# Single-use buffers for four expert loads, and all adaLN loads inside the trunk

## The chip, the cores and the metric

One core of a Trainium2 chip runs the whole kernel. The metric is device microseconds of one execution. TensorE (PE) multiplies, VectorE (DVE), ScalarE (ACT) and GpSimd (POOL) do the rest, SyncE (SP) issues most of the DMAs, and 16 DMA engines carry them.

## The reference

One layer of a diffusion backbone in fp32, width 2048, on two streams of 128 tokens each (context and latent):

```python
mods = silu(c) @ w_ada + b_ada                 # 2048 -> 6 x 2048, for both streams
h = rmsnorm(x, norm1_g) * (1 + sc1) + sh1
u_f, q, k, v, g_a, g_b = h @ w_in + b_in       # 2048 -> 8192
merged = sigmoid(g_a) * (fourier(u_f) @ w_fourier) + sigmoid(g_b) * (attention(q, k, v) @ w_na_o)
x1 = x + ga1 * (merged @ w_out)
h2 = rmsnorm(x1, norm2_g) * (1 + sc2) + sh2
# router: best of 4 groups, then the best 2 of its 4 experts; 16 experts in all
y = sum_e comb[:, e] * ((silu(h2 @ w_g[e]) * (h2 @ w_u[e])) @ w_d[e])
x2 = x1 + ga2 * y
out = rmsnorm(x2, final_norm_g)                # and k, v of the context stream
```

## The kernel before

**The trunk.** All weights are read once, in loads of 1 MB. The dense weights (w_in, w_na_o, w_fourier, w_out) are 96 loads, `l` = 0 to 95; each is two units of 12 matmuls (`unit`, L776): a weight is split into a high and a low part (ScalarE `high` L1302, VectorE `low` L1652, four units ahead), and hi*hi, lo*hi and hi*lo are added up for both samples. Loads 80 to 95 are w_out (`L_OUT` = 80). After each chunk of four of these VectorE (`read_chunk`, L1743) multiplies by the adaLN gate (`gab`), adds to `x1`, and makes `yt`. The adaLN weights are another 96 loads; 0 to 31 go another way, 32 to 95 are *groups* `ada_super(a)` (L760) of four matmuls, eight instructions in the profile, that add into bank 7. The loads of both kinds share a ring of four 1 MB buffers, `raw`, in the order of `ring_order` (L350). From load 18 on TensorE runs two groups after the first unit of every second load. `LATE_ADA = 5` (L346) keeps the last five groups, 91 to 95, out of this: they come last in the ring, ScalarE issues their loads during the last loads of the trunk (L1500, and L1525 for 95), and TensorE runs them in the seam.

**The seam** lies between the last matmul of load 95 and the first expert matmul. TensorE, from L1042: router matmuls of block 2 for both samples, transposes of `x1` for block 3 and sample 0, group 91, transposes for sample 1, router matmuls of block 3, groups 92 and 93, the rank matmuls (they wait for VectorE's `chosen`), groups 94 and 95. VectorE: gate product and sum for sample 0, then sample 1 (both wait for the whole load, L1748), `yt`, the inverse root mean square, the logits, `chosen`, `token_low(3)` for both samples (L1804, the low part `t_lo` of the tokens), the slot keys and `rounds` (how many rounds of 64 tokens an expert needs), the first `pick` tiles (L2041), and then, after group 95, the gate row `garow`. TensorE reads `rounds` into a register, waits for `pick` and all eight `t_lo`, and makes the slot rows (L1091) and the gathered tokens `xg` (L1080).

**The experts.** 16 experts in 8 pairs. Each pair has 16 gate/up loads (four quarters q, gate and up, two experts) and 8 down loads; 192 loads in all, numbered n = 0 to 191 in the order of use, unit u using loads 2u and 2u + 1. Loads 0 to 15 are the gate/up loads of pair 0. The first unit of its quarter 3 is unit 6, with loads 12 and 13. Eleven buffers (`MRAW`) are used in turn: slots 0 to 3 lie over `w_hi` and `w_lo`, 4 to 7 over `raw`, 8 to 10 are `mraw_g`, `mraw_x`, `mraw_y`. Load n goes to slot n mod 11 once load n - 11 has been used (`slot_free`, L512). TensorE raises `loads_used` when a load has been used.

SyncE issues all of these in program order, so whatever it waits for holds up everything behind it: loads 9 and 10 as soon as it is through with the trunk's loads, 8 after chunk 21, 0 and 2 after load 94 of the trunk, 1 and 3 after load 95, 4 to 7 when the four `raw` buffers are free of groups 92 to 95, then the value of `rounds`, and loads 11 to 191 by `slot_free`. At the end of its loop it waits for all eleven slots, and then issues the output's DMAs.

Regions of SBUF: A (32 KB a partition) holds `m_hi` and `m_lo` during the output projection, and then `xg`, `d_hi`, `d_lo`, `hidT`, `sg`, `hid`; F (32 KB) holds `x1`, and over its upper half `x1T` (the router's operand) and later `ga2b`.

## Time and profile before

| | us |
|---|---|
| median of 3 runs | 1212.66 |
| lowest, highest | 1212.19, 1212.76 |
| the profiled execution, its own time | 1213.01 |
| its span | 1211.2 |
| TensorE busy | 1125.0 (93%) |
| VectorE busy | 535.5 (44%) |
| ScalarE busy | 365.2 (30%) |
| data moved | 423.22 MB, mean 349 GB/s |

A busy TensorE is not one at its peak: matmul ends are modelled, and one that waits for nothing follows the one before it without a gap. In the windows of the rows below the columns are: stretch and its length, busy us and number of instructions of PE, PEld (weight load), DVE, ACT and POOL, then the granted TensorE clock as a share of 2.4 GHz, the mean busy share of the 16 DMA engines, and GB/s. In a timeline line the columns are start, duration, engine, source line, operation, output <- inputs, shapes, and the number of instructions merged. A "q" behind an engine is its sequencer, which issues DMAs. "Chain" is the work that ended last, followed back from the end.

### The profile page before, as it was taken

How to read it: one execution, taken by the hardware profiler on the slowest of the kernel's cores; microseconds unless marked ns; L12 is line 12 of the kernel's file. 1: busy time of each engine (PE TensorE's matmuls, PEld its weight loads, DVE VectorE, ACT ScalarE, POOL GpSimd, SP SyncE). 2: the span in 40 equal slices, each digit the busy share in tenths (PEclk: the TensorE clock that was granted, in tenths of full speed). 3: DMA queues.
4: the chain of work that ended last, by engine and by line, in shares of the span. 5: the costliest groups of instructions: out<-in, count | busy, mean ns of one | idle time of the engine just before them, and what ended most of it. 6: DMA issues, size and time to landing. Idle time of an engine off the chain costs nothing.

```text
span 1211.2 us, 14465 instructions
## 1 busy us (share of the span) xinstructions
PE 1125.0 (93%) x5577; PEld 686.6 (57%) x5577; DVE 535.5 (44%) x781; ACT 365.2 (30%) x512; POOL 54.7 (5%) x100
## 2 busy tenths in 40 slices
PE   5899999999999999999999999999999888988795
PEld 2575766777777777677788865443334233423231
DVE  0364575555455444454557654133324141514046
ACT  3342342444433333333345533311112011201023
POOL 0210100110000210000011100000000000000000
PEclk9899999999999999999999999899999999999998
DMA  9999978888877898888898798899999999999994
GB/s 359 384 386 374 361 263 321 295 293 287 286 281 284 308 351 322 310 316 314 317 331 260 225 367 360 363 422 423 423 423 422 423 423 422 423 423 424 423 411 171
DMA packets 114964, 423.22 MB, mean 349 GB/s; under 512 B 9088, under 2 KB 9264, under 8 KB 82640
## 3 DMA queue, kind: packets, MB, share of 16 engines
q1 hardware_dynamic: 101824, 388.52, 82.2%
q0 software_dynamic: 5424, 15.35, 4.9%
q10 hardware_dynamic: 7648, 18.42, 4.3%
q8 instruction: 45, 0.74, 0.2%
q14 instruction: 23, 0.19, 0.0%
HBM read 418.27 MB, written 3.98 MB: 349 GB/s over the span
## 4 chain that ended last, share of the span: by engine, by line
PE 66%; DMA 29%; DVE 2%; SPq 1%; issue 1%; ACT 1%; DVEq 0%
PE bank L791 13%; PE bank L793 13%; PE bank L792 12%; PE bank L1139 10%; DMA mraw<-in_w_exp_up 6%; PE bank L772 4%; DMA raw<-in_w_in 4%; DMA raw<-in_w_ada 4%; DMA mraw<-in_w_exp_gate 3%; PE bank L1169 3%; PE bank L1080 2%; DMA mraw_x<-in_w_exp_up 2%; DMA mraw_g<-in_w_exp_up 2%; DMA mraw_y<-in_w_exp_gate 2%; DMA mraw_g<-in_w_exp_down 2%; DMA mraw_y<-in_w_exp_up 2%
## 5 line engine op out<-in xcount | busy, mean ns | idle before, releaser
L1657 DVE TENSOR_TENSOR w_lo<-raw,w_hi 128x1024 fp32r<-128x1024 f32 x192 | 231.9, 1223 | 256.3 <-ACT w_hi L1310 255.0
L1310 ACT ACTIVATE w_hi<-raw 128x1024 fp32r<-128x1024 f32 x192 | 200.3, 1057 | 322.2 <-DMA raw<-in_w_in 160.9
L791 PE MATMUL bank<-w_hi,h_hi 128*128 128x512 f32 x512 | 206.9, 404 | 7.1 <-DVE uqkv L1740 5.7
L1139 PE MATMUL bank<-mraw,xg 128*64 128x512 f32 x768 | 193.9, 602 | 15.9 <-DMA mraw<-in_w_exp_gate 8.1
L792 PE MATMUL bank<-w_lo,h_hi 128*128 128x512 f32 x512 | 200.6, 392 | 0.0
L793 PE MATMUL bank<-w_hi,h_lo 128*128 128x512 f32 x512 | 200.2, 391 | 0.0
L1139 PEld LDWEIGHTS bank<-mraw,xg 128*64 128x64 f32 x768 | 61.9, 138 | 118.8 <-issue 114.2
L791 PEld LDWEIGHTS bank<-w_hi,h_hi 128*128 128x128 f32 x512 | 96.7, 189 | 47.9 <-issue 15.7
L793 PEld LDWEIGHTS bank<-w_hi,h_lo 128*128 128x128 f32 x512 | 96.5, 189 | 21.0
L792 PEld LDWEIGHTS bank<-w_lo,h_hi 128*128 128x128 f32 x512 | 96.7, 189 | 18.3
L1169 PE MATMUL bank<-mraw,hidT 128*64 128x512 f32 x320 | 83.3, 596 | 16.2 <-DMA mraw<-in_w_exp_down 13.8
L2112 DVE SCALAR_TENSOR_TENSOR d_lo<-bank,slot_w,d_hi 128x512 fp32r<-128x512 f32 x32 | 23.9, 747 | 160.3 <-ACT d_hi L1603 159.6
L1603 ACT ACTIVATE d_hi<-bank,slot_w 128x512 fp32r<-128x512 f32 x32 | 22.0, 688 | 229.0 <-PE bank L1169 142.0
L2124 DVE TENSOR_TENSOR bank<-bank,ga2b 128x512 f32<-128x512 f32 x64 | 41.5, 694 | 80.0 <-PE bank L1210 79.9
L772 PE MATMUL bank<-raw,cpad 128*32 128x512 f32 x512 | 63.5, 606 | 4.5 <-DMA raw<-in_w_ada 4.5
L1169 PEld LDWEIGHTS bank<-mraw,hidT 128*64 128x64 f32 x320 | 26.7, 137 | 60.5 <-issue 56.1
L791 PE MATMUL bank<-w_hi,m_hi 128*128 128x512 f32 x128 | 50.9, 398 | 0.0
L793 PE MATMUL bank<-w_hi,m_lo 128*128 128x512 f32 x128 | 50.0, 390 | 0.0
L792 PE MATMUL bank<-w_lo,m_hi 128*128 128x512 f32 x128 | 49.9, 390 | 0.0
L756 PE MATMUL bank<-araw,cpad 128*32 128x512 f32 x256 | 35.1, 657 | 13.6 <-DMA araw<-in_w_ada 13.6
L2059 DVE TENSOR_TENSOR xg<-bank,rbi 128x512 f32<-128x512 f32 x32 | 21.9, 685 | 52.9 <-PE bank L1080 52.9
L1139 PE MATMUL bank<-mraw_x,xg 128*64 128x512 f32 x88 | 40.0, 597 | 1.8 <-DMA mraw_y<-in_w_exp_gate 1.6
(283 smaller groups left out, 1311.0 us busy)
## 6 DMA issues: line engine op xcount, KB each, us to landing
raw<-in_w_in SPq DMA_DIRECT2D x64, 1024.0 KB, 8.8
raw<-in_w_ada SPq DMA_DIRECT2D x59, 1024.0 KB, 7.5
mraw<-in_w_exp_up SPq DMA_DIRECT2D x49, 1024.0 KB, 20.9
mraw<-in_w_exp_gate SPq DMA_DIRECT2D x47, 1024.0 KB, 20.9
mraw<-in_w_exp_down SPq DMA_DIRECT2D x40, 1024.0 KB, 20.8
araw<-in_w_ada SPq DMA_DIRECT2D x64, 512.0 KB, 10.4
raw<-in_w_out ACTq DMA_DIRECT2D x12, 1024.0 KB, 9.2
raw<-in_w_na_o SPq DMA_DIRECT2D x8, 1024.0 KB, 8.1
```

The costliest lines, as they stand in the source:

```text
L756: last = nc.tensor.matmul(bank[7 - b % 2][32 * g:32 * g + 32], cpad[:, 2 * j + g % 2], araw[:, n % ARAW, g], start=j == 0, stop=j == 7)
L772: last = nc.tensor.matmul(bank[7][32 * g:32 * g + 32], cpad[:, k], raw[:, n % RAW, g], start=k == 0, stop=k == KD - 1)
L791: nc.tensor.matmul(o, hi[:, k, s], wh, start=k == first, stop=False)
L792: nc.tensor.matmul(o, hi[:, k, s], wl, start=False, stop=False)
L793: last = nc.tensor.matmul(o, lo[:, k, s], wh, start=False, stop=k == final)
L1080: last = nc.tensor.matmul(out[:, kk * EPG * CAP:(kk + 1) * EPG * CAP], (t_hi, t_lo)[part][:, s, k * P:(k + 1) * P], pick[:, s, g * EPG:(g ...
L1139: last = nc.tensor.matmul(out[x * CAP:(x + 1) * CAP], xg[:, q * LOAD_K + kk, e * CAP:(e + 1) * CAP], slab(slot)[:, kk * COL:(kk + 1) * COL ...
L1169: last = nc.tensor.matmul(bank[first_bank + n][x * CAP:(x + 1) * CAP], hidT[:, i % 2, k, x * CAP:(x + 1) * CAP], slab(slot)[:, n * COL:(n ...
L1310: nc.scalar.activation(w_hi[:, u % AHEAD], r, ACT.Copy).then_inc(hi_ready, 1)
L1657: v.tensor_tensor(w_lo[:, u % AHEAD], r, w_hi[:, u % AHEAD].bitcast(F32), ALU.subtract).then_inc(raw_done[n % RAW], 4)
L2112: v.scalar_tensor_tensor(out=d_lo[:, c % 2], in0=bank[first_bank + n][:], scalar=slot_w[:, i:i + 1], in1=d_hi[:, c % 2].bitcast(F32), op0= ...
L2124: v.tensor_tensor(bank[out + s][:], bank[out + s][:], ga2b[:, s, cols], ALU.mult).then_inc(y_scaled, 1)
```

## The change

1. `LATE_ADA` becomes 0. Groups 91 to 95 run inside the trunk: two groups after the first unit of loads 76, 78 and 80 (before: one, 90, at load 76 and none later). ScalarE issues no adaLN load any more.
2. The last dense load (95) is multiplied by `last_load`: all twelve matmuls of sample 0, then all of sample 1, each raising `unit_used` by one. VectorE's product for each sample waits for its own half.
3. TensorE's order in the seam: transposes of block 3, sample 0; router of block 2; transposes for sample 1; router of block 3; rank matmuls.
4. `token_low(3)` is split: sample 0 ahead of the rank reduction, sample 1 behind the first `pick` tiles.
5. Loads 8 to 11 go to four buffers that are used once: two in A + 16 KB (over `m_lo`, free after load 93 and load 95), two in F + 16 KB (over `x1T`, free after the router). They count their landing on the semaphores of `part_landed`. All other loads have a *place* in the ring (n below 8, else n - 4); place p waits for the load at place p - 11.
6. SyncE's order: 13, 14, 12 (after chunk 21), 8 (after load 93 of the trunk), 4 to 7 (after the conversions of dense loads 92 to 95), 0 and 2, 1 and 3, 9, then 10 and 11 after the router, the value of `rounds`, 15, and the rest as before.
7. At the end of its loop SyncE first waits for the last of ScalarE's squares (`x2_squared`), then for the eleven places.
8. `cmp` moves from A + 24 KB to A.

```diff
+        mraw_a = place("mraw_a", [P, 2, LOAD_K * COL], A + 16 * KB)
+        mraw_f = place("mraw_f", [P, 2, LOAD_K * COL], F + 16 * KB)
-        cmp = place("cmp", [P, NS * 5, EPG, 2 * EPG], A + 24 * KB)
+        cmp = place("cmp", [P, NS * 5, EPG, 2 * EPG], A)
-        LATE_ADA = 5
+        LATE_ADA = 0
+        ONCE, ONCE_AT = 4, 2 * RAW
+        def single_use(n):
+            return ONCE_AT <= n < ONCE_AT + ONCE
+        def place_in_ring(n):
+            return n if n < ONCE_AT else n - ONCE
+        def load_at(place):
+            return place if place < ONCE_AT else place + ONCE
...
             def slot_free(r, n):
-                if n >= MRAW:
-                    sp.wait_ge(loads_used, used_value(r, n - MRAW))
+                place = place_in_ring(n)
+                if place >= MRAW:
+                    sp.wait_ge(loads_used, used_value(r, load_at(place - MRAW)))
...
-                first_gate_up_load(2 * RAW + 1)
-                first_gate_up_load(2 * RAW + 2)
+                first_gate_up_load(13)
+                first_gate_up_load(14)
                 sp.wait_ge(chunk_read, reads(21))
-                first_gate_up_load(2 * RAW)
+                first_gate_up_load(12)
+                sp.wait_ge(unit_used, 2 * L_ALL - 4)
+                first_gate_up_load(8)
+                for n in range(RAW):
+                    sp.wait_ge(raw_done[n], 8 * (RING_LOADS // RAW))
+                    first_gate_up_load(RAW + n)
                 for n in (0, 2, 1, 3):
                     sp.wait_ge(unit_used, 2 * L_ALL - 2 + n % 2 * 2)
                     first_gate_up_load(n)
-                for n in range(RAW):
-                    sp.wait_ge(raw_done[n], 8 * (RING_LOADS // RAW))
-                    first_gate_up_load(RAW + n)
+                first_gate_up_load(9)
+                sp.wait_ge(route_done, NS)
+                first_gate_up_load(10)
+                first_gate_up_load(11)
                 sp.wait_ge(rounds_ready, 1)
                 sp.reg_load(rounds_end, rounds[0:1, 0:1])
-                slot_free(r, MRAW)
-                first_gate_up_load(MRAW)
-                for up in range(2):
-                    gate_up_loads(r, 0, 3, up)
+                slot_free(r, 15)
+                first_gate_up_load(15)
...
+                sp.wait_ge(x2_squared, r * 8 + 8)
+                sp.sem_inc(slots_freed, 1)
...
+            last_load(L_ALL - 1)
+            x1_transposes(3, 0)
             for s in range(NS):
                 router(2, s)
-            x1_transposes(3, 0)
-            ada_super(91)
             x1_transposes(3, 1)
             for s in range(NS):
                 router(3, s).then_inc(route_done, 1)
-            for a in (92, 93):
-                ada_super(a)
             pe.wait_ge(chosen_ready, 1)
...
-            for a in (94, 95):
-                ada_super(a)
...
-                if L_ALL <= l + RAW < L_ALL + LATE_ADA:
-                    ada_super_load(act, 96 - LATE_ADA + l + RAW - L_ALL)
...
-            ada_super_load(act, 95)
...
-                dve.wait_ge(unit_used, 2 * l + 2)
+                dve.wait_ge(unit_used, 2 * l + 2 - (l == L_ALL - 1))
...
-            token_low(3)
+            token_low(3, (0,))
...
             build_pick(0, EPG)
+            token_low(3, (1,))
```

## Rows read from the trace of the kernel before

**Rows 1.** The page: GB/s that the DMA engines moved, in 40 slices.

```profile
GB/s 359 384 386 374 361 263 321 295 293 287 286 281 284 308 351 322 310 316 314 317 331 260 225 367 360 363 422 423 423 423 422 423 423 422 423 423 424 423 411 171
```

**Rows 2.** Windows by stage: length, busy us by engine, clock, DMA share, GB/s.

```profile
600.00:700.00 100.00, 100.00 (x471) 83.28 (x470) 66.67 (x73) 51.19 (x62) 9.64 (x18) 1.00 0.85 278
...
766.00:844.00 78.00, 78.00 (x387) 32.20 (x385) 24.55 (x38) 17.27 (x30) 0.00 (x0) 1.00 1.00 414
844.00:1187.00 343.00, 301.75 (x1381) 119.38 (x1379) 105.88 (x168) 44.63 (x75) 0.00 (x0) 1.00 1.01 421
```

**Rows 3.** The chain of waits (start us, us, what) from the seam on.

```profile
713.21 7.16 DMA raw<-in_w_ada
720.41 1.98 PE bank L772 x8
...
727.80 7.09 PE bank L1139 x32
...
754.83 4.45 PE bank L1251 x32
...
844.23 17.08 DMA mraw<-in_w_exp_up
```

**Rows 4.** SyncE: its DMA issues (start us, us, what), the first expert loads.

```profile
702.45 0.33 SPq L509 DMA_DIRECT2D mraw<-in_w_exp_gate  x1
...
751.49 0.33 SPq L509 DMA_DIRECT2D mraw_g<-in_w_exp_up  x1
752.00 0.33 SPq L509 DMA_DIRECT2D mraw_x<-in_w_exp_gate  x1
...
755.43 10.96 SPq L509 DMA_DIRECT2D mraw<-in_w_exp_up  x2
...
766.06 0.33 SPq L509 DMA_DIRECT2D mraw<-in_w_exp_up  x1
```

**Rows 5.** Windows around load 23, columns as above.

```profile
764.00:766.00 2.00, 2.00 (x12) 0.62 (x10) 0.00 (x0) 0.00 (x0) 0.00 (x0) 0.92 0.06 25
```

**Rows 6.** TensorE in the trunk: a timeline row, two windows, a row of waits.

```profile
580.67 1.92 PE L772 MATMUL bank<-raw,cpad 128*32 128x512 f32 x16
...
594.67:613.85 19.18, 19.18 (x89) 15.87 (x86) 14.40 (x18) 8.10 (x8) 0.00 (x0) 1.00 0.84 311
569.55:593.67 24.12, 24.12 (x116) 18.28 (x113) 9.25 (x9) 9.17 (x9) 0.00 (x0) 1.00 0.91 328
...
PE bank L772 <- DMA raw<-in_w_ada: 4.5, 4, 1.7
```

**Rows 7.** Timeline of the seam; idle time before it in brackets.

```profile
708.85 0.69 DVE L1781 TENSOR_TENSOR gab<-gab,bank 128x512 f32<-128x512 f32 x1 [9.47 <-PE bank L793]
...
710.18 0.68 DVE L1781 TENSOR_TENSOR gab<-gab,bank 128x512 f32<-128x512 f32 x1
...
716.77 1.93 DVE L1804 TENSOR_TENSOR t_lo<-yt,t_hi 128x512 fp32r<-128x512 f32 x2
...
718.61 0.19 DVE L2027 TENSOR_REDUCE rt<-bank 128x16 f32<-128x32 f32 x1
...
719.68 0.75 DVE L2041 TENSOR_TENSOR pick<-cst_route,key 128x256 fp32r<-128x256 f32 x2
...
722.28 1.22 PE L1091 MATMUL bank<-pick,rr 128*128 128x256 f32 x4
```

**Rows 8.** Windows where the granted clock fell, and before the first.

```profile
716.00:720.00 4.00, 2.03 (x18) 0.90 (x14) 3.79 (x13) 0.45 (x2) 0.00 (x0) 1.00 0.96 320
720.00:723.40 3.40, 2.99 (x13) 1.32 (x14) 1.38 (x4) 0.00 (x0) 0.00 (x0) 0.50 0.98 410
...
757.50:764.30 6.80, 6.80 (x23) 3.43 (x25) 0.00 (x0) 2.41 (x6) 0.00 (x0) 0.50 0.88 360
```

**Rows 9.** Timeline of the end: last square, first output DMA.

```profile
1201.13 0.19 ACT L1584 ACTIVATION_READ_ACCUMULATOR sg<-x 128x1 f32 x1
...
1204.20 0.36 SPq L581 DMA_DIRECT2D out<-x  x1
```

64 lines of the change are left out of this document (43 added, 21 removed).

## The prediction

> **What bounds the kernel now.** I read the page's slices first: data moves at 225 to 386 GB/s in the first 26 slices and stands at 422 to 424 GB/s from slice 27 nearly to the end [rows 1]. The stages say which side is the limit. From 600 to 700 us TensorE is busy all of the time and the DMA engines move 278 GB/s: the trunk is TensorE's. From 844 to 1187 us the DMA engines have a share of 1.01 at 421 GB/s and TensorE idles 41 of 343 us: the experts are the load stream's [rows 2]. The chain of waits shows the same turn: up to 844 us it is TensorE back to back, broken at one place in the seam by an adaLN load (713.21, 7.16 us) with the matmuls of its group behind it, and from 844.23 it hops from one expert load to the next [rows 3]. One load of 1 MB (1.0486 MB) at 421 GB/s is 2.49 us.
>
> So two things can move the end: the number of bytes still to fetch after the moment at which the stream last ran dry, and that moment. It can be found. SyncE issued load 22 at 755.43 and load 23 at 766.06, one wait of 10 us between them; load 23 reuses the buffer of load 12, so it waits for unit 6, the first of the two units of the pair's last quarter [rows 4]. The DMA engines meanwhile ran out: share 0.06 from 764 to 766 us [rows 5], against 1.00 in the stage from 766 to 844 and 1.01 in the one after it [rows 2]. Hence the **anchor**: end = end of unit 6 (766.0) + 169 loads (23 to 191) + the tail. 766.0 + 169 x 2.49 = 1187, which is where the stream ends.
>
> **The change part by part.**
>
> *Five adaLN groups into the trunk.* Before, groups 91 to 95 ran in the seam, four of them while TensorE waited for VectorE anyway. Now they lie among the dense matmuls of loads 76 to 81. The stretch 594.67 to 613.85 holds 84 dense matmuls and no group: 228 ns each. The stretch 569.55 to 593.67 holds 96 and one pair of groups: 24.12 - 96 x 0.228 = 2.2 us for a pair, 1.1 us for one. Its own row says 1.92 us for a pair [rows 6]. Five groups are 4.8 to 5.5 us, and nothing hides them where TensorE is busy all of the time [rows 2]. I take +5.0: the breaks between dense runs, which make the difference, grow by two only. Their 5 MB also move into the trunk, where 278 GB/s leave room.
>
> *The seam.* Before, from VectorE's first product after the last matmul (708.85) to the first slot-row matmul (722.28) it is 13.4 us [rows 7]. (a) The last load is now multiplied sample by sample, so the product and sum of sample 0 run under sample 1's matmuls; VectorE gains 710.18 - 708.85 = 1.3 us. TensorE has four transposes and 16 router matmuls (about 2.2 us) ahead of the last transposes, which could start after 1.8 us, so about 1.0 of the 1.3 survives. (b) Only sample 0 of the last t_lo pair (1.93 us for two) stays ahead of the rank reduction, which now starts at about 717.8 on the old clock instead of 718.61: 0.8 us. The other half, 0.97 us, comes behind the first pick tiles, and TensorE waits for it before the slot rows. (c) Before, the first pick tiles were done at 719.68 + 0.75 = 720.43, but the slot rows came only at 722.28, behind adaLN groups 94 and 95; that cover goes. After: 720.43 - 708.85 = 11.6, less 1.0, less 0.8, plus 0.97, plus 0.3 for the semaphore, is 11.1 us. The seam is shorter by **2.3 us** (bounds: 1.8 if only 0.5 of (a) survives, 2.6 if all of it does). cmp moves into room that the output projection has left: nothing. ScalarE issues five DMAs fewer, none of them on the path: nothing.
>
> *The clock.* At 720 us the granted clock fell to 0.50, the 1.2 GHz level, for 3.4 us, after four microseconds in which TensorE was busy for 2.0, with the rank's small matmuls and group 94 [rows 8]. Dense work had come back at 720.41 [rows 3]; the clock returned 3.0 us later, but only 1.1 us after the slot rows had begun, because group 95 used up the rest. Without groups 92 to 95 TensorE has only the router's and the rank's small matmuls from the end of the trunk to the restart, so I expect the clock low at the restart, and 3.0 us of the path's own work at half speed instead of 1.1: +(3.0 - 1.1)/2 = **+1.0**. Bounds: -0.5 if it does not fall, and +2.9 if it stays low for 6.8 us, as in the other stretch, 757.5 to 764.3 [rows 8]. The Trainium skill, in "TensorE: Matmul & The Clock Gate", Part 1, says that "the default state is throttled, and activity releases the throttle"; it speaks against taking filler work out of a gap, and the row at 720 us agrees. By the rule alone, with no row for the length, one could only say that this term is not below nothing.
>
> The second low stretch follows the 4.45 us of slot-weight matmuls (754.83) [rows 3], which the change leaves alone; dense work from 759.3 to 764.3 ran at half speed and lost 2.5 us. I keep it: 0, with bounds of -2.5 (clock stays up) and +1.
>
> *Four more loads in flight.* Loads 8 to 11 go to single-use buffers, loads 12 to 14 take the ring's places 8 to 10, so loads 15 to 22 wait for loads 0 to 7 instead of 4 to 11. SyncE's order is 13, 14, 12, then 8, 4, 5, 6, 7, 0, 2 while the last loads of the trunk are multiplied (before: first 0 and 2, at 702.45 [rows 4]), then 1, 3, 9 at its end, and 10, 11 after the router. From load 23 on the wait is the same as before: place 19 waits for place 8, which is load 12. So the stream now stands still earlier, with load 22 landed some 10 us sooner, and restarts at the same instruction of TensorE. Worth **0**. Does a first use come late? Ten loads, 8 to 3 in SyncE's order plus 9, need 25 us from about 700, so to 725; 10 and 11 land near 730. The first unit (loads 0 and 1) starts 5.5 us after the slot rows (727.80 before [rows 3]), so at about 731, and units 4 and 5 twenty us later: no wait. Load 8's semaphore wait now stands ahead of loads 4 to 7 on SyncE; it costs nothing for the same reason, and if the cover were gone 2.49 us a load.
>
> *The end of SyncE's loop.* It now waits for the last square before it checks the eleven places. The last square's accumulator is read at 1201.13 + 0.19 = 1201.3. Between two expert loads whose buffers are free, issued at 751.49 and 752.00, a check takes at most 0.51 - 0.33 = 0.18 us [rows 4]; eleven are 2.0 us and bring SyncE to 1203.3, and the output's DMA goes out at 1204.20 [rows 9]. Covered by 0.9 us; without that it would be on the path one for one.
>
> **Sum**: 5.0 - 2.3 + 1.0 + 0 + 0 = **+3.7 us** at the end of unit 6, and so at the end. The profiled execution took 1213.01 us around its span of 1211.2; 1213.01 + 3.7 = 1216.7. It stands 0.35 above the median of the runs, 1212.66, so the predicted median is 1216.4.
>
> **The rivals.**
>
> *A, the forecast*: 1216.4. Its own range, with the terms' bounds not all at one end, is 1214.2 to 1219.
>
> *B, the clock stays up or returns early.* Where the clock falls need not be the same twice. With -0.5 at the restart and -1 in the second stretch the sum is 5.0 - 2.3 - 0.5 - 1.0 = +1.2: 1213.9. For it: the clock was still 1.00 up to 720 us [rows 8], although the trunk's dense matmuls had ended at 708.8. Against it: what kept TensorE at work then, groups 91 to 94, is gone.
>
> *C, the trunk starves.* Loads 76 to 81 now have two dense loads of lead instead of four, while x1 and the gate and norm rows come in. TensorE waited 4.5 us in 4 places, at most 1.7, for an adaLN load in the whole kernel [rows 6]. Two waits of that size give +3.4: 1219.8. Against it: 29 earlier pairs ran with the same lead, and those 4 waits are all there were, one of them in the seam.
>
> *D, the head start lasts, and the kernel gets faster.* Mechanism: four loads that are fetched ahead no longer have to be fetched behind the anchor: 4 x 2.49 = 10.0 us, so 1216.4 - 10.0 = 1206.4. It would decide if load 23 could be issued while the DMA engines still worked on loads up to 22, so if unit 6 ended before about 763 us on the old clock. The idle 764 to 766 us say that it does not [rows 5], and in the changed kernel the queue empties earlier still. The Trainium skill's "DMA: Bandwidth & Descriptors", Rules for kernel authors, advises to issue a DMA early and wait on its semaphore late; by that rule the time would be this 1206.4, and the row at 764 us says why it is not: early is worth nothing ahead of a place where the queue runs dry anyhow.
>
> *E, the change does not do what it says*: TensorE has slack in the trunk that no row shows, and the five groups cost nothing there: 3.7 - 5.0 = -1.3, so 1211.4. Against it: 100.00 us busy in 100 [rows 2].
>
> **How the numbers follow.** Chances: A 0.55, B 0.20, C 0.10, D 0.08, E 0.07. The predicted time is A's. D and E lie below the range, and little of C above it, so 1212.5 to 1219.8 leaves out less than 2 in 10. A measurement of this kernel can tell 0.2%, 2.4 us, from no change. Faster by more than that: D and a rest, 0.10. Within it: B, E and the low edge of A, 0.30. Slower: the rest of A and C, 0.60.
>
> **What the profile after would show.** The last dense matmul ends near 713.8 instead of 708.8, and three adaLN pairs stand after 590 us. The first slot-row matmul comes 11.1 us after it. The clock is 0.50 over the restart. SyncE issues load 22 near 750 and load 23 only at about 770, with the DMA engines idle for over 10 us before; after it the share is 1.0 to the end. The prediction is wrong if the DMA engines are busy when load 23 is issued, if TensorE waits in the trunk, or if load 23 goes out at 766 or sooner.

## The result, and the profile after

The changed kernel took 1219.41 us (median of 6 runs, 1217.31 to 1222.08), the kernel before beside it 1212.71 (1210.48 to 1213.85): a ratio of 1.0059, 95% interval 1.0045 to 1.0073. It is slower, by 6.7 us, where +3.7 was forecast. The profiled execution took 1219.20 us, its span is 1217.4 (before 1211.2: +6.2).

The page's slices still rise to 423 GB/s from slice 27 on, behind a deeper hole in slice 26 (245, before 363 [rows 1]):

```profile
GB/s 360 384 386 375 361 250 329 294 285 285 281 285 277 327 355 318 304 330 324 308 400 286 181 371 343 245 423 423 423 423 423 424 424 422 423 423 423 423 407 177
```

Windows (stretch, length, busy us of PE, PEld, DVE, ACT, POOL, then granted clock, DMA share, GB/s) of the trunk, of the stretch in it that matters, of the experts' start, and of the load stream, which answer to [rows 2] and [rows 5]:

```profile
600.00:700.00 100.00, 97.11 (x450) 77.18 (x449) 62.06 (x69) 46.23 (x57) 9.64 (x18) 0.98 0.84 290
612.00:648.00 36.00, 35.00 (x166) 27.29 (x165) 16.60 (x17) 13.44 (x16) 3.23 (x6) 1.00 1.03 399
732.00:756.00 24.00, 24.00 (x141) 14.20 (x142) 12.07 (x23) 11.71 (x22) 0.00 (x0) 0.98 0.80 323
756.00:772.00 16.00, 16.00 (x84) 7.57 (x82) 2.44 (x9) 2.41 (x6) 0.00 (x0) 0.89 0.32 133
772.00:850.00 78.00, 78.00 (x387) 32.32 (x385) 24.56 (x38) 17.27 (x30) 0.00 (x0) 1.00 0.99 412
850.00:1193.00 343.00, 301.87 (x1381) 119.02 (x1378) 105.72 (x167) 44.43 (x75) 0.00 (x0) 1.00 1.01 421
...
764.00:772.00 8.00, 8.00 (x42) 4.18 (x43) 0.00 (x0) 2.41 (x6) 0.00 (x0) 0.79 0.00 0
```

In the trunk TensorE is no longer busy all of the time (97.11 of 100 us, clock 0.98). From 612 to 648 the DMA engines have a share of 1.03: the room that I had seen in 278 GB/s is gone there. There had been little of it: the kernel before, in the same stretch, has a share of 0.95 at 315 GB/s, and the 278 GB/s of its 100 us stood beside a share of 0.85 [rows 2].

```profile
612.00:648.00 36.00, 36.00 (x167) 29.89 (x166) 23.20 (x25) 16.98 (x21) 5.37 (x10) 1.00 0.95 315
```

Behind 756 the stream dries up, 0 GB/s from 764 to 772, and from 772 on it runs as before.

SyncE's DMA issues, which answer to [rows 4]: the first three expert loads, the load before load 22, load 22 and load 23.

```profile
613.52 7.40 SPq L499 DMA_DIRECT2D raw<-in_w_out  x2
621.12 0.36 SPq L535 DMA_DIRECT2D mraw_x<-in_w_exp_gate  x1
621.52 0.43 SPq L535 DMA_DIRECT2D mraw_y<-in_w_exp_up  x1
621.99 0.43 SPq L535 DMA_DIRECT2D mraw_g<-in_w_exp_gate  x1
...
749.04 3.25 SPq L535 DMA_DIRECT2D mraw<-in_w_exp_gate  x2
752.48 0.33 SPq L535 DMA_DIRECT2D mraw<-in_w_exp_up  x1
...
772.40 0.33 SPq L535 DMA_DIRECT2D mraw_g<-in_w_exp_up  x1
```

Load 23 goes out at 772.40 instead of 766.06 [rows 4], +6.3, and the span is longer by 6.2. The anchor of the prediction (the end moves as load 23 moves) holds to 0.1 us; what was wrong lies ahead of it. The trunk shows it (timeline; idle time before a row in brackets):

```profile
627.99 0.39 ACTq L499 DMA_DIRECT2D raw<-in_w_out  x1
...
644.98 1.06 ACT L1353 ACTIVATE w_hi<-raw 128x1024 fp32r<-128x1024 f32 x1 [7.77 <-DMA raw<-in_w_out]
...
646.14 2.36 DVE L1697 TENSOR_TENSOR w_lo<-raw,w_hi 128x1024 fp32r<-128x1024 f32 x2 [7.60 <-ACT w_hi L1353]
...
648.42 0.68 DVE L1823 TENSOR_TENSOR gab<-gab,bank 128x512 f32<-128x512 f32 x1
649.13 0.69 DVE L1829 TENSOR_TENSOR x<-x,gab 128x512 f32<-128x512 f32 x1
...
649.88 0.66 PE L1015 MATMUL bank<-cst_all,x 128*128 128x128 f32 x4 [2.89 <-DVE x L1829]
```

Dense load 85, of w_out, is issued by ScalarE at 627.99 and lands 17.0 us later. ScalarE waits 7.77 us for it, VectorE 7.60 us behind ScalarE, the product and the sum of x1 are queued behind the late `w_lo` on VectorE, and TensorE's transposes of x1 wait 2.89 us for these. Then the clock falls. Windows of that low stretch and of the two others, which answer to [rows 8]:

```profile
651.20:654.60 3.40, 3.40 (x10) 2.62 (x9) 3.40 (x5) 0.72 (x2) 2.15 (x4) 0.50 0.56 191
...
722.90:733.10 10.20, 5.17 (x23) 5.07 (x24) 7.62 (x21) 3.49 (x11) 0.00 (x0) 0.50 1.01 421
767.20:770.60 3.40, 3.40 (x10) 0.98 (x8) 0.00 (x0) 1.91 (x4) 0.00 (x0) 0.51 0.00 0
```

The seam's timeline, which answers to [rows 7]: VectorE's product of the last sample, `pick`, the second half of `t_lo`, the first slot-row matmul, the first expert matmuls.

```profile
718.18 0.69 DVE L1823 TENSOR_TENSOR gab<-gab,bank 128x512 f32<-128x512 f32 x1 [1.21 <-PE bank L843]
...
727.64 0.75 DVE L2083 TENSOR_TENSOR pick<-cst_route,key 128x256 fp32r<-128x256 f32 x2
728.31 1.00 DVE L1846 TENSOR_TENSOR t_lo<-yt,t_hi 128x512 fp32r<-128x512 f32 x1
729.41 1.19 PE L1137 MATMUL bank<-pick,rr 128*128 128x256 f32 x4 [2.95 <-DVE t_lo L1846]
...
735.66 4.91 PE L1184 MATMUL bank<-mraw,xg 128*64 128x512 f32 x21
```

Five marks of TensorE's timeline carry the rest of this text: the adaLN pair that starts near 580 us [rows 6], the end of the last dense matmul, the first slot-row matmul, the first expert matmul, and the span. "Pair to dense" is the time from the start of that pair to the dense end, "rest" is the span less the first expert matmul. Times are those of the profiled execution, one for each kernel. Up to that pair all of these kernels do the same work, and yet it starts between 580.07 and 583.70, so the columns of differences are safer than those of times. The start in the kernel before is 580.67 [rows 6], in after and in e1:

```profile
580.16 1.92 PE L806 MATMUL bank<-raw,cpad 128*32 128x512 f32 x16
...
580.14 1.92 PE L807 MATMUL bank<-raw,cpad 128*32 128x512 f32 x16
```

| kernel | pair to dense | dense end | slot rows | first expert | span | rest | median | ratio to before, 95% |
|---|---|---|---|---|---|---|---|---|
| before | 128.1 | 708.8 | +13.5 | +19.0 | 1211.2 | 483.4 | 1212.71 | |
| after | 138.0 | 718.2 | +11.3 | +17.5 | 1217.4 | 481.7 | 1219.41 | 1.0059 (1.0045 to 1.0073) |
| e1 | 133.3 | 713.4 | +11.4 | +17.6 | 1212.5 | 481.5 | 1215.25 | 1.0035 (1.0022 to 1.0047) |
| e16 | 134.0 | 716.9 | +11.3 | +17.5 | 1216.0 | 481.6 | 1217.76 | 1.0040 (1.0027 to 1.0053) |
| e17 | 133.3 | 714.7 | +11.3 | +17.7 | 1213.8 | 481.5 | 1215.51 | 1.0027 (1.0014 to 1.0039) |
| e12 | 128.1 | 708.9 | +13.1 | +18.4 | 1210.8 | 483.5 | 1212.45 | 1.0005 (0.9992 to 1.0018) |
| e13 | 129.9 | 711.6 | +13.1 | +18.7 | 1213.8 | 483.6 | 1214.97 | 1.0010 (0.9992 to 1.0029) |
| e14 | 147.9 | 730.2 | +11.7 | +18.8 | 1232.1 | 483.1 | 1233.59 | 1.0153 (1.0130 to 1.0175) |
| e2 | 137.9 | 718.0 | +11.6 | +18.8 | 1220.0 | 483.2 | 1219.74 | 1.0064 (1.0051 to 1.0077) |
| e3 | 137.2 | 718.2 | +13.4 | +19.6 | 1219.5 | 481.7 | 1221.39 | 1.0084 (1.0064 to 1.0103) |
| e4 | 128.1 | 709.2 | +12.3 | +17.7 | 1207.1 | 480.3 | 1210.71 | 0.9994 (0.9986 to 1.0003) |
| e5 | 133.3 | 714.1 | +11.3 | +17.6 | 1213.6 | 481.9 | 1215.36 | 1.0037 (1.0024 to 1.0049) |
| e6 | 128.1 | 711.8 | +14.2 | +19.8 | 1213.7 | 482.1 | 1212.34 | 1.0009 (0.9997 to 1.0021) |
| e7 | 128.1 | 708.5 | +16.0 | +22.0 | 1214.2 | 483.7 | 1215.67 | 1.0033 (1.0020 to 1.0045) |
| e8 | 128.1 | 708.5 | +15.1 | +20.7 | 1212.3 | 483.2 | 1212.89 | 1.0004 (0.9992 to 1.0017) |
| e9 | 133.3 | 716.2 | +13.2 | +18.5 | 1216.1 | 481.5 | 1216.92 | 1.0038 (1.0025 to 1.0051) |
| e15 | 133.3 | 714.3 | +13.9 | +19.2 | 1215.2 | 481.7 | 1215.01 | 1.0021 (1.0008 to 1.0034) |
| e10 | 129.0 | 710.9 | +11.6 | +16.9 | 1210.2 | 482.4 | 1210.23 | 0.9985 (0.9971 to 1.0000) |
| e11 | 129.0 | 710.7 | +10.6 | +15.9 | 1208.0 | 481.5 | 1209.64 | 0.9977 (0.9963 to 0.9991) |

From the pair to the dense end it is 128.14 or 128.15 us in the six kernels with five groups in the seam and no wait in the trunk (before, e4, e6, e7, e8, e12), and 133.25 to 133.28 in the five with no group in the seam and no wait in the trunk (e1, e5, e9, e15, e17). So five groups in the trunk cost 5.1 us, and one costs 0.9 (e10, e11).

### The profile page after: what moved, and what is told of

It reads as the page before. It is cut to its first block, busy times and chain, and to the rows that moved or that the text cites. A ratio compares the mean times of both kernels' runs of the same rounds, so it can differ in the third digit from the quotient of the medians.

```text
span 1217.4 us, 14461 instructions
## 1 busy us (share of the span) xinstructions
PE 1122.0 (92%) x5577; PEld 685.5 (56%) x5577; DVE 535.9 (44%) x781; ACT 365.2 (30%) x512; POOL 54.8 (4%) x100
## 4 chain that ended last, share of the span: by engine, by line
PE 66%; DMA 28%; DVE 2%; SPq 1%; ACT 1%; issue 1%; DVEq 0%
PE bank L825 13%; PE bank L826 12%; PE bank L827 12%; DMA mraw<-in_w_exp_up 11%; PE bank L1184 10%; PE bank L806 5%; DMA raw<-in_w_in 4%; DMA mraw<-in_w_exp_gate 3%; DMA mraw<-in_w_exp_down 3%; PE bank L1213 3%; PE bank L1126 2%; DMA raw<-in_w_ada 2%; DMA mraw_y<-in_w_exp_gate 2%; DMA raw<-in_w_out 1%; PE bank L1234 1%; PE bank L1253 1%
## 5 line engine op out<-in xcount | busy, mean ns | idle before, releaser
L1184 PE MATMUL bank<-mraw,xg 128*64 128x512 f32 x720 | 184.9, 597 | 14.4 <-DMA mraw<-in_w_exp_gate 6.7
L825 PEld LDWEIGHTS bank<-w_hi,h_hi 128*128 128x128 f32 x512 | 96.7, 189 | 50.2 <-DVE uqkv L1780 14.6
L1184 PEld LDWEIGHTS bank<-mraw,xg 128*64 128x64 f32 x720 | 58.0, 136 | 110.8 <-issue 106.3
L1184 PE MATMUL bank<-mraw_g,xg 128*64 128x512 f32 x96 | 45.4, 617 | 2.5 <-DMA mraw_x<-in_w_exp_up 1.3
L827 PE MATMUL bank<-w_hi,m_lo 128*128 128x512 f32 x120 | 47.4, 395 | 0.0
```

The costliest lines, as they stand in the source:

```text
L825: nc.tensor.matmul(o, hi[:, k, s], wh, start=k == first, stop=False)
L827: last = nc.tensor.matmul(o, lo[:, k, s], wh, start=False, stop=k == final)
L1184: last = nc.tensor.matmul(out[x * CAP:(x + 1) * CAP], xg[:, q * LOAD_K + kk, e * CAP:(e + 1) * CAP], slab(2 * unit + x)[:, kk * COL:(kk + ...
```

## Experiments: the wait in the trunk

**e1, the first three expert loads later.** In the changed kernel SyncE comes to them at 621 and not at 606, since its dense load 83 now waits for a `raw` buffer of an adaLN group in the trunk. Here they wait for dense load 88.

```diff
+                sp.wait_ge(unit_used, 2 * (L_OUT + 9))
                 first_gate_up_load(13)
                 first_gate_up_load(14)
```

> The changed kernel, with one wait more: SyncE issues the first three expert loads (13, 14, 12) only when load 88 of the trunk has been multiplied, not at 621 us. Theory 'collision': in the changed kernel these three loads come between x1's 2 MB and dense loads 83 to 85, and dense load 85 lands so late that TensorE stands still for 3.3 us at 646.6 us and then runs 3.4 us at the half clock. Without them there it loses neither: the last dense matmul ends near 714, and the time is 4 to 5 us below the changed kernel's, about 1214.7 (+2 us against the kernel before). Rival 'lead': it is the adaLN loads in the ring, which leave dense loads 82 to 85 two loads of lead instead of four; then the wait stays and the time stays near 1219.4 (+6.7).

The trunk's wait and the low clock behind it are gone: dense work ends at 713.4 and not at 718.2, and the median falls by 4.2 us (by the ratios to the kernel before, each in its own batch, by 2.9). Seam and rest are the changed kernel's. SyncE's issues up to dense load 83 stand where they stood in the changed kernel (613.48 and 613.52 for the last two), so the rival that blamed the adaLN loads in the ring falls. From the pair to the dense end it is 5.1 us more than in the kernel before, the price of the five groups, and 4.7 us less than in the changed kernel, the price of the wait and of the low clock.

**e16 and e17, the dose.** The same wait ahead of the third load alone (e16), and ahead of the second and third (e17).

```diff
 e16
                 sp.wait_ge(chunk_read, reads(21))
+                sp.wait_ge(unit_used, 2 * (L_OUT + 9))
                 first_gate_up_load(12)
 e17
                 first_gate_up_load(13)
+                sp.wait_ge(unit_used, 2 * (L_OUT + 9))
                 first_gate_up_load(14)
```

> The changed kernel with the third of its three early expert loads held as in e1 and the other two at 621 as they were. Theory (the wait is the backlog: each load is 1 MB, 2.49 us of the queue): dense load 85 lands 2.5 us earlier than in the changed kernel, near 642.5; TensorE's wait falls from 3.05 to 0.5 us and the clock may stay up; dense work done 714.2 to 715.8 (after's time base), time 1215.8 to 1217.4. Rival (the wait is set by any expert load in that place, or by x1's 2 MB): as the changed kernel, 1219.4.

> The changed kernel with the second and the third early expert load held as in e1, the first alone at 621. Theory (backlog): no wait left, dense work done at 713.7, time as e1, 1215.3. Rival (any expert load there): 1219.4, or between.

Microseconds from the issue of dense load 85 to its landing, from the DMA view of its issue alone: of after, of e16, of e17 and of e1, in this order.

```profile
raw<-in_w_out ACTq DMA_DIRECT2D x1, 1024.0 KB, 17.0
```

```profile
raw<-in_w_out ACTq DMA_DIRECT2D x1, 1024.0 KB, 14.6
```

```profile
raw<-in_w_out ACTq DMA_DIRECT2D x1, 1024.0 KB, 13.7
```

```profile
raw<-in_w_out ACTq DMA_DIRECT2D x1, 1024.0 KB, 11.8
```

With three, two, one and none of the expert loads in flight beside it, load 85 takes 17.0, 14.6, 13.7 and 11.8 us. TensorE's wait at the transposes of x1 is 2.89 us in after, 0.55 in e16,

```profile
650.22 0.66 PE L1016 MATMUL bank<-cst_all,x 128*128 128x128 f32 x4 [0.55 <-DVE x L1830]
```

and none in e17 and e1. Only after's is followed by a low clock. From the pair to the dense end the four take 138.0, 134.0, 133.3 and 133.3 us: the third load costs the changed kernel 4.0 us (2.3 of waiting, the rest of low clock), the second 0.8, the first nothing. That is one profile of each. The medians share it out otherwise (1.7 us for the third load, 2.2 for the second, 0.3 for the first), and e16's missed its range by 0.4 us at the slow side, so the shares are less sure than the sum. In its profile the wait was what was expected.

The queues of the DMA engines say how (packets, MB, share of 16 engines; q1 is SyncE's, q10 ScalarE's, q0 GpSimd's). After, 628 to 644:

```profile
q1 hardware_dynamic: 628, 3.51, 55.7%
q10 hardware_dynamic: 863, 1.70, 28.5%
q0 software_dynamic: 320, 1.05, 17.8%
```

e1, 628 to 639:

```profile
q0 software_dynamic: 316, 1.04, 48.0%
q10 hardware_dynamic: 873, 1.72, 44.0%
q1 hardware_dynamic: 211, 0.40, 9.8%
```

Urgent dense loads on ScalarE's queue get 28.5% of the engines, while SyncE's queue gets 55.7%, and all but the last of dense load 83 on it (0.40 MB in e1's row) is expert loads, needed some 130 us later. The Trainium skill says in "DMA: Bandwidth & Descriptors", Issuing engines are not separate DMA queues, that DMAs of all issuing engines run on the same 16 DMA engines and interleave; by these rows the trace agrees.

**e12 and e13, the control in the kernel before.** The same meeting put into the kernel before. e12's count had long been reached, so its loads went out at 606.24 as ever: it is a repetition of the kernel before (ratio 1.0005), and it tests nothing. e13 has the right count.

```diff
 e12
+                sp.wait_ge(unit_used, 2 * (L_OUT - 8))
                 first_gate_up_load(2 * RAW + 1)
 e13
+                sp.wait_ge(unit_used, 2 * (L_OUT + 9) - 17)
                 first_gate_up_load(2 * RAW + 1)
```

> The kernel before with one wait more: its first three expert loads are issued when the trunk's 8th-last load before the output projection is used, near 617, that is 3 us behind the 2 MB of x1 and 6 us ahead of dense load 85, instead of at 606. This puts the changed kernel's meeting of transfers into the kernel before and leaves all else. My theory (the meeting makes the trunk wait): TensorE waits 1.5 to 3 us near 642 to 650 for a dense slab and the granted clock halves for 3.4 us behind it, +1.6: 1214 to 1216.5. Rival (the changed kernel's wait came from its longer trunk and the ring's order of adaLN loads): within 0.5 of before.

> The kernel before with one wait more on SyncE: the first three expert loads go out at 617, which is 3 us behind x1's 2 MB and 6 us ahead of dense load 85's issue, instead of at 606. Nothing else is changed. My theory (their meeting with x1's loads makes the trunk wait): TensorE waits 1.5 to 3 us for a dense slab between 640 and 650, the granted clock halves for 3.4 us behind it (+1.6): dense work done near 712 to 713, time 1214.5 to 1216.5. Rival (the changed kernel's wait comes from its ring order or its longer trunk): dense work done at 708.7, time within 0.5 us of before.

e13's timeline, SyncE's issue and TensorE's transposes of x1:

```profile
618.05 0.34 SPq L509 DMA_DIRECT2D mraw_x<-in_w_exp_gate  x1
...
644.94 0.66 PE L966 MATMUL bank<-cst_all,x 128*128 128x128 f32 x4 [1.55 <-DVE x L1788]
```

The kernel before, whose trunk did not wait here, now waits 1.55 us at the same place for the same releaser, load 85 taking 15.6 us instead of 11.9. From the pair to the dense end it takes 129.9 us, 1.7 more than before. The median is 2.0 us over that of before in the same batch, but the ratio's interval reaches below 1.0 (0.9992 to 1.0029), and the clock did not fall behind this wait, as the theory had it. The meeting alone makes a wait, and the changed kernel's is larger: there dense load 83 shares the time as well, issued 15 us later than before. That last part is argued, not shown.

**e14, the three loads earlier.** The changed kernel with two of the loads ahead of dense load 82 in SyncE's queue and the third ahead of load 83.

```diff
                     ada_super_load(sp, A_SUPER + l - L_LOOP)
+                if l == SP_DENSE - 3:
+                    first_gate_up_load(13)
+                    first_gate_up_load(14)
+                if l == SP_DENSE - 2:
+                    sp.wait_ge(chunk_read, reads(21))
+                    first_gate_up_load(12)
                 dense_load(sp, l + 1)
```

> The changed kernel with its first two expert loads issued ahead of dense load 82 (near 608.7) and the third behind it, ahead of dense load 83 (near 614), that is 8 and 3 us ahead of x1's loads, where the kernel before has all three 8 us ahead. Theory: no wait in the trunk, dense work done near 713.7, time as e1, 1215.3. Rival (any place ahead of 650 in the changed kernel's longer trunk meets its adaLN loads, and the wait stays): dense work done at 716 to 718.4, time 1217 to 1219.5.

```profile
634.73 1.06 ACT L1355 ACTIVATE w_hi<-raw 128x1024 fp32r<-128x1024 f32 x1 [13.45 <-DMA raw<-in_w_out]
...
647.58 1.06 ACT L1355 ACTIVATE w_hi<-raw 128x1024 fp32r<-128x1024 f32 x1 [9.87 <-DMA raw<-in_w_out]
```

Both theories missed by far: ScalarE waits 13.45 and 9.87 us for dense loads, dense work ends at 730.2, and the time is 1233.6. I had copied the distance to x1's loads from the kernel before and overlooked SyncE's queue: there the expert loads stand behind its last dense load, here ahead of it. Dense load 82 was issued at 615.68 behind 2 MB in its own queue, with x1's 2 MB on GpSimd's, and took 19.0 us. Here the order of issues in one queue weighed more than the distance to another queue's loads.

## Experiments: the parts of the change

**e2, no single-use buffers, and e3, the adaLN groups alone.** e2 is the changed kernel with `ONCE` = 0 and the kernel before's order of loads. e3 is the kernel before with `LATE_ADA` = 0 and the five groups taken out of the seam.

> The changed kernel without the four single-use buffers: all expert loads in the ring of eleven, in SyncE's order of before except that loads 4 to 7 stay ahead of 0 to 3; adaLN groups, seam and the rest as changed. Theory 'anchor': the four buffers are worth nothing, since load 23 waits for load 12 either way and the DMA engines are idle then; the time is the changed kernel's, 1219.4, within 1.5 us. Rival 'head start': four loads fetched ahead are four fewer to fetch later, so that without them the kernel is up to 10 us slower, 1222 to 1229.

> The kernel before with only the adaLN part of the change: groups 91 to 95 in the trunk, none in the seam; seam order, last load, t_lo and buffers as before. Theory 'collision': +5 us for five groups, the same wait for a late dense load and the half clock behind it (+4.7 at most; the first three expert loads are issued at the same place), -1.6 in the seam (slot rows right behind the first pick tiles), +0.5 to +1 from the clock at the restart: +4 to +9, about 1220, and a seam of about 11.8 us from the end of the last dense matmul to the slot rows. Rival 'the seam order is what costs': then this is below the changed kernel, at 1216 or less.

e2 is as slow as the changed kernel (1.0064 and 1.0059): the four buffers are worth nothing, as forecast. e3 shows the groups' move alone at +9.4 us in medians, a little over its range of +4 to +9, with the dense end at 718.2 as in after and a wait of 2.21 us at the same transposes; the rival that blamed the order of the seam falls. Its seam was to take 1.6 us less; its slot rows come 13.4 us after the dense end, and the granted clock stands at 0.50 for 13.7 us (721.6 to 735.3). The reordered seam then gains 2.1 us in slot rows (e3 against after).

**e8, the reordered seam alone** (kernel before, adaLN groups still in the seam), and with it **e6** (e8 with the slot weights later) and **e7** (e6 with the four buffers). All three, and e10 and e11, keep the changed kernel's end of SyncE's loop and its place of `cmp`; e8's rest of 483.2 us against 483.4 shows no cost of either.

```diff
-            for l in range(L_LOOP, L_ALL):
+            for l in range(L_LOOP, L_ALL - 1):
...
+            last_load(L_ALL - 1)
+            x1_transposes(3, 0)
             for s in range(NS):
                 router(2, s)
-            x1_transposes(3, 0)
             ada_super(91)
```

> The kernel before with the reordered seam alone: last dense load by sample, last transposes ahead of the router, low parts split, SyncE's order of the expert loads 0 to 3; five adaLN groups still in the seam, ring of 11. My theory, from e6 (which differs from e4 by the same edit): adaLN group 95's slab is landed late, behind the expert loads, and TensorE's last adaLN matmuls hold the slot rows up; from the end of the dense work to the slot rows 14.3 us instead of 13.4, time 1 to 1.6 us over before, 1212.5 to 1213.5. Rival (the reorder gains its 2.3 us whatever stands in the seam): 1209.

> The kernel before with its last five adaLN groups still in the seam, its ring of 11 and its order of expert loads, but with the reordered seam of the change (last unit by sample, transposes ahead of the router, the low parts split) and with the slot weights and gate-row broadcasts behind the first unit of pair 1. Trunk as before, dense work done at 708.7; the seam is shorter by up to 1 us than before's 13.4; then as e4_before_slot_weights_later. My theory: 1209 to 1211, that is, e4 or up to 1 us under it. Rival (the end is set by the queue's rate alone once it never runs dry): same as e4 to 0.5 us, 1210.7.

> As e6_late_ada_new_order_ring with the four buffers used once added, their loads (8 to 11) behind the first slabs of the ring. Transfers are in flight four loads (10 us at 2.49 us) earlier than the ring allows, and the ring's first load that waits for an expert unit is load 15 instead of 11. If the end is the queue's (issue of the first waiting load plus the loads left at 2.49 us), this is worth up to 4 us against e6: 1206 to 1207. Rival 1 (TensorE's own order sets the place of unit 6 and the queue waits for it anyway): same as e6 to 1 us. Rival 2 (the earlier loads delay the raw slabs of the seam's last adaLN groups): slower than e6 by 1 to 3 us.

Slot rows come 15.1 us after the dense end in e8, 14.2 in e6, 16.0 in e7, against 13.5 before. e7's row, with `pick` ready at 719.26:

```profile
718.51 0.75 DVE L2092 TENSOR_TENSOR pick<-cst_route,key 128x256 fp32r<-128x256 f32 x2
...
722.69 1.94 PE L806 MATMUL bank<-raw,cpad 128*32 128x512 f32 x8 [4.37 <-DMA raw<-in_w_ada]
```

TensorE waits 4.37 us for the slab of group 95, whose load ScalarE can issue only when the dense loop is over, behind the expert loads. The reorder is worth something only if this slab is out of the way: e8's time is that of before (1.0004), a little better than my theory; e6 is 1.1 us over its batch's before and above its range of 1209 to 1211, e7 is 4.5 over and 9 above its theory. e7's second rival holds: group 95's load takes 9.9 us from issue to landing in e7 and 8.1 in e6, so earlier expert loads delay the urgent adaLN slab.

**e4 and e5, the slot weights later.** The anchor is unit 6. The slot-weight matmuls and the gate rows stand ahead of it (4.45 us [rows 3]); both kernels move them behind the first unit of pair 1, e4 in the kernel before, e5 in e1.

```diff
-                    if q == 2:
-                        pe.wait_ge(xg_scaled, r * 32 + 8)
-                        ...
-                        last.then_inc(slot_w_done, 1)
...
                 for i in range(1, PAIRS):
                     gate_up(i, 0, 0)
+                    if i == 1:
+                        ga2_rows(2)
+                        ga2_rows(3)
+                        pe.wait_ge(xg_scaled, r * 32 + 8)
+                        ...
+                        last.then_inc(slot_w_done, 1)
```

> The kernel before with another order on TensorE and ScalarE only: the 4.45 us of slot-weight matmuls and the four gate-row broadcasts (1.15 and 0.67 us) stand no longer between quarters 2 and 3 of pair 0; the broadcasts of rows 0 and 1 come after quarter 3, those of rows 2 and 3 and the slot weights after the first unit of pair 1. No work is left out. Theory 'anchor': the end is the end of unit 6 plus 169 loads at 2.49 us, so what is taken from ahead of unit 6 comes off the end: -4.45 - 1.15 = -5.6 and up to 2.5 more from the clock; 1207, range 1204.5 to 1209. Rival 'bytes': the end is set by all bytes from the seam on or by TensorE's whole work, neither of which changes; 1212.7.

> The changed kernel with its first three expert loads held until dense load 85 is used (as in e1_first_three_later) and, in addition, the slot weights and the gate-row broadcasts behind the first unit of pair 1. In e1 the four single-use buffers cannot pay, because the load behind them waits for unit 6 of pair 0 at about 767, where the queue had run dry. My theory (the end is that unit plus 169 loads at 2.49 us): here unit 6 ends 5 to 6 us earlier in relation to the seam, load 23 goes out near 761, and the time is e1 less 5, about 1210. Rival (what e4 showed of the kernel before: the transfers between 760 and 800 then move at 406 to 409 GB/s and give most of it back): e1 less 1 to 2, about 1213.5.

Both missed. In e5 load 23 goes out 5.4 us earlier (762.28, e1 767.68), yet the time is e1's. Its GB/s in 40 slices of 1 us from 760:

```profile
GB/s 0 0 0 147 336 393 459 418 434 401 459 418 426 426 434 426 418 434 262 0 0 0 131 238 434 426 442 401 156 344 418 426 442 401 369 393 410 459 418 270
```

The stream starts earlier, dries up again at 779 to 782 and slackens once more at 788. Moving TensorE's work does not take it away; the last place at which the stream runs dry moves behind it. The sum that held in all of these kernels is another one: rest is 481.5 to 483.7 us in 18 of the 19, whatever stands ahead, so a kernel of this family ends some 482 us after its first expert matmul. With the old place of the slot weights it is 483.1 to 483.7 where the second low stretch lasts 6.8 us, and 481.5 to 481.7, once 482.4 (e10), where it lasts 3.4. With the slot weights later it is 480.3 in e4 and 482.1 in e6, whose low stretch lasts 3.4, and 481.9 in e5 and 483.7 in e7, where it lasts 6.8: a gain of 1.2 us in two profiles and none in the two others. In medians e4 is the kernel before to 0.1%, so no worth of the later slot weights is shown.

**e9 and e15, fillers in the seam.** e1 with matmuls of 512 columns whose output nothing uses: e9 four while TensorE waits for `chosen` and six while it waits for `pick`, e15 two and three.

```diff
                 router(3, s).then_inc(route_done, 1)
+            for _ in range(4):
+                nc.tensor.matmul(bank[1][:], ident, x1[:, 0, 0:COL], start=True, stop=True)
```

> The changed kernel as in e1_first_three_later, with ten matmuls of 512 columns that nothing uses on TensorE in the seam: four while it waits for the chosen experts, six while it waits for the slot rows. In e1 the granted clock is at half from 717.4 to 727.6, and the expert work begins at half clock. My theory for the term of the clock (+0.7 to +1.0 us in the seam, and what the slow start costs behind it): with TensorE kept busy the clock stays up, and the time falls by 1 to 2.5 us against e1's 1215.3. Rival: the fillers delay the router's rank matmuls or the broadcasts, or the queue sets the end whatever the clock is: within 0.5 us of e1, or slower by up to 2.

> e1 with five fillers (two while TensorE waits for the chosen experts, three while it waits for the slot rows) instead of e9's ten; at 0.88 us each they fit in the two waits of 2.8 and 3.9 us. Theory (the half clock in the seam costs what the restart shows, 0.7 to 1.0 us, and nothing behind it): slot rows 11.1 us after the dense work, first expert matmul 16.4 after it instead of e1's 17.3, time 0.5 to 1 us under e1: 1214.5. Rival (the seam's clock has no share in the time): as e1 to 0.2 us.

Windows of e9 (the second set of fillers), then of e15:

```profile
724.00:729.30 5.30, 5.30 (x18) 2.67 (x17) 4.33 (x13) 0.00 (x0) 0.00 (x0) 1.00 1.02 427
```

```profile
717.90:728.10 10.20, 10.20 (x22) 5.65 (x23) 7.60 (x25) 2.45 (x7) 0.00 (x0) 0.50 1.01 419
```

Ten fillers kept the clock at 1.00 through the seam: from the slot rows to the first expert matmul 5.3 us instead of e1's 6.2. But they held the slot rows up by 1.7 us, and e9's rival stands: no gain. Five did not keep the clock up, ran at half speed themselves and took twice their time: slot rows 2.5 us later than e1's. e15's median is e1's to 0.3 us, and its expected gain of 0.5 to 1 us isn't there in the profile; the two intervals overlap. The Trainium skill's rule of "TensorE: Matmul & The Clock Gate", Part 1, which the prediction quoted, is borne out by e9's clock; e15's five fillers left the clock low all the same. At the price of ten fillers the rule buys nothing here.

**e10 and e11, four groups back in the seam.** The reordered seam with groups 92 to 95 where TensorE waits anyway and group 91 in the trunk, so that all four slabs are loaded from the dense loop; e10 with the ring of 11, e11 with the four buffers.

```diff
-        LATE_ADA = 0
+        LATE_ADA = 4
...
                 router(3, s).then_inc(route_done, 1)
+            for a in (92, 93):
+                ada_super(a)
...
+            for a in (94, 95):
+                ada_super(a)
```

> The changed kernel's seam with the ring of 11, and four of the five adaLN groups back in the seam: 92 and 93 where TensorE waits for the chosen experts, 94 and 95 where it waits for the slot rows. Group 91 stays in the trunk, so that group 95's slab is loaded from the dense loop and not behind the expert loads. In e1 these two waits last about 2.8 and 3.9 us, and two groups take 1.85. My theory (groups are free in the seam's waits, and TensorE's being busy keeps the granted clock at 1.00): trunk +1 us against before (dense work done at 709.7), slot rows 11.1 to 11.5 us later, first expert matmul 5.0 later, near 726: 1207.5 to 1209. Rival 1 (slab 95 lands late all the same): 1210 to 1212. Rival 2 (first three expert loads now collide with x1's as in the changed kernel): 1212 to 1214.

> As e10_four_late_ring with the four buffers used once, in the order of e7. My theory (the end is the first expert matmul plus a constant 481.5 us, whichever load is ahead in the queue): as e10 to 0.7 us, if adaLN slabs are not late. Rival, from e7: one more expert load ahead of the seam's adaLN slabs delays them, slower than e10 by 2 to 4 us.

e11's rows: `pick`, and TensorE's first slot-row matmul, which waits for VectorE and not for a slab; then a window of its seam.

```profile
719.53 0.75 DVE L2089 TENSOR_TENSOR pick<-cst_route,key 128x256 fp32r<-128x256 f32 x2
...
721.31 0.70 PE L1141 MATMUL bank<-pick,rr 128*128 128x256 f32 x4 [1.10 <-DVE t_lo L1852]
...
713.00:721.30 8.30, 6.60 (x57) 3.53 (x56) 7.29 (x27) 3.40 (x9) 0.00 (x0) 1.00 1.01 421
```

The groups are useful fillers: the slot rows wait for VectorE and for none of them, and come 10.6 us after the dense end, the first expert matmul 15.9 (before 19.0), for 0.9 us more of trunk (129.0 against 128.1). The clock stays at 1.00 in e11's seam, but in e10, with the same groups, it is at 0.50 for 3.4 us, and in e12, which repeats the kernel before, it stays up where before's fell: with groups in the seam the low stretch is short or absent, and one profile does not tell which. e11 takes 1209.64 us, ratio 0.9977 (0.9963 to 0.9991): the one kernel here whose interval lies wholly below the kernel before, by 2.4 us in medians of the same batch; the changed kernel stands 9.8 us above it. e10's interval ends at 1.0; the two differ by 0.6 us, which is no proof of a worth of the buffers. e10 came out 1.2 us above its expected range and in that of its first rival, though no slab was late (its slot rows wait 1.10 us for `t_lo`, as in e11); e11 came out where e10 put it.

## Why the prediction was right or wrong

The forecast was right in its sign and its place and too small by 3.0 us: the anchor and the other terms held within 1.7 us, and one term of the sum was mis-sized, by a wait that it put at nothing. In the profiled executions:

| term | forecast | measured |
|---|---|---|
| five groups in the trunk | +5.0 | +9.3 at the dense end; +9.8 from the pair near 580 us: 5.1 for the groups (e1), 4.7 for a wait (2.9) and the low clock behind it |
| dense end to slot rows | -2.3 | 13.5 to 11.3: -2.2 |
| slot rows to first expert | +1.0 | 5.5 to 6.3: +0.7 |
| first expert to the end | 0 | 483.4 to 481.7: -1.7 |
| four buffers | 0 | e2: 0.3 us slower without them, within the intervals |
| sum | +3.7 | 9.3 - 2.2 + 0.7 - 1.7 = 6.1; span +6.2 |

*The step that failed* is the sentence "Their 5 MB also move into the trunk, where 278 GB/s leave room", and with it the +5.0 that the sum took for this part: the wait behind those 5 MB was put at nothing. The price of the matmuls was right (5.1 against 5.0). The 278 GB/s hid that the trunk's DMA engines are nearly full for 36 us of the 100 already in the kernel before (share 0.95 from 612 to 648), with x1, the gate and norm rows, the dense loads and three expert loads; the changed kernel's are full (1.03). It is the share, 0.85 in the same row, that tells of room, and it left 15 us of the 100 for five loads of 2.49. I followed the five moved loads but not what is queued behind them: on SyncE, dense load 83 and the first three expert loads slipped by 15 us, into just that stretch. Rival C, with a chance of 0.10, named the place, a trunk that starves while x1 and the gate rows come in, and the prediction's own sign of being wrong, that TensorE waits in the trunk, came true. C's cause did not: it blamed the short lead of loads 76 to 81 behind the adaLN loads in the ring, and priced two waits for adaLN loads at 3.4 us. What came late is dense load 85, on ScalarE's queue, and e1 takes the wait away with the ring as it is. That C's time, 1219.8, is 0.4 us from the measured one is luck. Its counter-argument, 29 earlier pairs with the same lead, looked at pairs where no expert loads were in flight.

*The seam* held to 0.1 us as a sum, its clock to 0.3. Its two parts did not hold: the cover of groups 94 and 95 was to fall away for 1.5 us and the new order to gain 0.8, while e3, without the groups and in the old order, is at 13.4 us as before, and the new order gains 2.1 on it. The two misses cancel, which is luck. The prediction has 0.3 us for a semaphore; in the changed kernel the slot rows start 0.1 us behind the end of `t_lo` (729.31 to 729.41). That the low stretch would outlast the restart was right (3.7 us past the slot rows, forecast 3.0); it lasted 10.2 us in all. The anchor held to 0.1 us, with load 23 at 772.40, which is 2.4 us later than the forecast's "about 770" because the trunk was; the last dense matmul ended at 718.2 where 713.8 was forecast. The stream was idle ahead of it, so rival D (the head start lasts) falls, and e2 confirms it. The advice of the Trainium skill, "DMA: Bandwidth & Descriptors", Rules for kernel authors, to issue early, which the prediction weighed, did harm in a second way that I had not seen: an early load shares the engines with an urgent one. Rival E falls with e1's 5.1 us. Rival B had the second low stretch right in kind (3.4 instead of 6.8 us, -1.7 where B had -1) and the first wrong. I had set the term of the second stretch to 0 with -2.5 as its bound; the table's rest column says that 6.8 or 3.4 us is worth 1.7.

*What stays open*: the profile before waited for an adaLN load at 568 us and reached the pair near 580 us 0.5 us later than after's did; without that its span would lie 6.7 us below after's, as the medians do. Each profile is one execution, and runs of one kernel spread over up to 8.6 us (e6), so agreement to tenths deserves little weight. Why the second low stretch lasts 6.8 us in some kernels and 3.4 in others is not known. How the 1.55 us of e13 becomes 2.89 us in the changed kernel was not tested by itself. Why e4 gains less than its one profile shows is open too.

## What to carry over

When a load moves into a busy stretch, list everything that its queue issues behind it, and lay each of those transfers over the DMA share of the stretch in which it will then run, not over the mean GB/s of the stage. A transfer that nobody needs for 130 us is best issued behind the urgent ones, both in its own queue and in time. And work that only has to be done sometime is best placed where an engine waits anyway: the four groups in the waits of e11's seam held nothing up, while the five in the trunk cost 5.1 us, and a seam without them ran for 10.2 to 13.7 us at the low clock.

## What the runs showed of the hardware

- The granted clock fell to 0.50 behind TensorE's waits of 2.89 us (after), 2.83 (e2) and 2.21 (e3) in the trunk, for 3.4 us each time, and did not behind waits of 1.55 (e13) and 0.55 us (e16). Across a seam without adaLN groups it stayed low for 10.2 to 13.7 us (not in e9, with its ten fillers), across a seam with four or five groups in it for 3.4 us, once 6.8 (e7), or not at all.
- A 1 MB load took 17.0, 14.6, 13.7 and 11.8 us with three, two, one and no expert loads of 1 MB on the other queue, and another 19.0 us behind 2 MB in its own (e14).
- DMA engines with a share of 0.95 to 1.03 moved 315 to 399 GB/s in the trunk (612 to 648 us), where the experts' stream moves 421 at 1.01: a low rate is no sign of room.
- Between two profiles of kernels whose first 580 us do the same work, the place of a given matmul differs by up to 3.6 us. The three latest (e6, e9, e16) are those in which the clock was low for 3.4 us near 121 us as well.
